# Expert weights in 4 MB transfers over a ring of four 32 KB places, in place of 2 MB transfers over nine 16 KB places

## The reference

```python
def expert(args):
    xb, e = args
    gu = (xb @ w_gu[e] + b_gu[e]).astype(f32)
    gate, up = jnp.split(gu, 2, axis=-1)
    gate = jnp.minimum(gate, SWIGLU_LIMIT)
    up = jnp.clip(up, -SWIGLU_LIMIT, SWIGLU_LIMIT)
    act = (up + 1.0) * gate * jax.nn.sigmoid(SWIGLU_ALPHA * gate)
    return act.astype(x.dtype) @ w_down[e] + b_down[e]
```

## Time and profile before

| | |
|---|---|
| median of 3 runs | 1506.49 us (1506.26 to 1506.98) |
| the profiled execution, time | 1506.73 us |
| its span, first to last instruction | 1505.0 us |
| PE busy / weight loads | 1466.1 us (97%) / 733.1 us (49%) |
| VectorE, ScalarE, GpSimd busy | 446.8, 344.2, 107.2 us |
| gate and up pieces | 128 transfers of 2048 KB, median 34.7 us from issue to landing |
| down pieces | 64 transfers of 2048 KB, median 35.9 us |
| bytes read from HBM | 491.19 MB (10^6 bytes) |
| granted TensorE clock, mean | 0.998 |

### The profile page before, as it was taken

One profiled execution on the slowest core, in us unless ns is written; L12 is line 12 of the kernel. 1 busy time (PEld: TensorE's weight loads), 2 busy tenths in 40 slices (PEclk: granted clock), 3 DMA queues, 4 the chain that ended last, 5 costly groups with the idle time before them and its releaser, 6 DMA issues.

```text
span 1505.0 us, 21866 instructions
## 1 busy us (share of the span) xinstructions
PE 1466.1 (97%) x8602; PEld 733.1 (49%) x8602; DVE 446.8 (30%) x918; ACT 344.2 (23%) x863; POOL 107.2 (7%) x95
## 2 busy tenths in 40 slices
PE   9999999999999999999999999999999999999997
PEld 7777776556777764333333333333333333333332
DVE  3653778776410137201101111111111101101113
ACT  1224215631210023212212112122112111211213
POOL 1003231010503301000000000000000000000000
PEclk9999999999999999999999999999999999999999
DMA  6346697546369767999999999999999999999996
GB/s 214 112 165 181 218 291 247 180 135 197 100 213 297 287 275 286 422 418 430 427 428 427 429 429 427 430 427 430 427 430 427 430 426 431 426 430 427 430 427 263
DMA packets 110574, 507.75 MB, mean 337 GB/s; under 512 B 12548, under 2 KB 49012, under 8 KB 85844
## 3 DMA queue, kind: packets, MB, share of 16 engines
q1 hardware_dynamic: 103840, 499.64, 82.9%
q10 hardware_dynamic: 6676, 7.29, 1.6%
HBM read 491.19 MB, written 15.72 MB: 337 GB/s over the span
## 4 chain that ended last, share of the span: by engine, by line
PE 67%; DMA 21%; DVE 3%; ACT 1%; issue 1%; DVEq 0%; SPq 0%; ACTq 0%
DMA wGU<-in_w_gu 21%; PE ps L2491 16%; PE ps L1950 12%; PE ps L2496 8%; PE ps L2259 4%; PE ps L2432 4%; PE ps L1966 3%; PE ps L2479 3%; PE ps L2483 3%; PE ps L2276 2%; PE ps L2289 2%; PE ps L2397 2%; PE ps L2413 1%; DVE up L1843 1%; DVE up L1842 1%; PE ps L2034 1%
## 5 line engine op out<-in xcount | busy, mean ns | idle before, releaser
L2491 PE MATMUL ps<-wGU,xe 128*64 128x512 f32 x1536 | 343.7, 595 | 15.7 <-DMA wGU<-in_w_gu 15.7
L2496 PE MATMUL ps<-wD,aT 128*64 128x512 f32 x1024 | 226.8, 595 | 0.0
L2491 PEld LDWEIGHTS ps<-wGU,xe 128*64 128x64 f32 x1536 | 108.4, 137 | 237.9 <-issue 211.3
L1950 PE MATMUL ps<-xT,ring 128*128 128x288 f32 (+1 forms) x848 | 179.6, 409 | 0.7 <-PEq L200 0.7
L1839 DVE TENSOR_SCALAR sg<-sg 128x512 f32<-128x512 f32 x32 | 13.7, 427 | 558.2 <-ACT sg L1280 558.2
L1950 PEld LDWEIGHTS ps<-xT,ring 128*128 128x128 f32 (+1 forms) x848 | 126.0, 172 | 44.6 <-issue 3.6
L2496 PEld LDWEIGHTS ps<-wD,aT 128*64 128x64 f32 x1024 | 71.4, 137 | 133.0 <-issue 126.2
L1280 ACT ACTIVATE sg<-ps 128x512 f32<-128x512 f32 x32 | 19.1, 597 | 487.2 <-PE ps L2479 487.2
L1229 ACT ACTIVATE xe<-ps,lnT 128x64 f32<-128x64 f32 x262 | 81.1, 420 | 1.2 <-PE ps L2406 1.2
L402 PE MATMUL ps<-xT,ring 128*128 128x288 f32 x320 | 78.1, 407 | 0.0
L1296 ACT COPY ysb<-ps 64x512 f32<-64x512 f32 x64 | 37.1, 579 | 155.5 <-PE ps L2496 154.8
(11 more groups left out here) (487 smaller groups left out, 1419.4 us busy)
## 6 DMA issues: line engine op xcount, KB each, us to landing
wGU<-in_w_gu SPq DMA_DIRECT2D x128, 2048.0 KB, 34.7
wD<-in_w_down SPq DMA_DIRECT2D x64, 2048.0 KB, 35.9
ring<-in_w_in SPq DMA_DIRECT2D x21, 2048.0 KB, 9.1
out<-hst SPq DMA_DIRECT2D x8, 1024.0 KB, 5.7
ringS<-in_ssd_proj SPq DMA_DIRECT2D x4, 2048.0 KB, 8.4
wbuf<-prompt_A_rows ACTq DMA_DIRECT2D x16, 384.0 KB, 3.8
out<-Sb SPq DMA_DIRECT2D x2, 2048.0 KB
ring<-in_hg_proj SPq DMA_DIRECT2D x2, 2048.0 KB, 8.6
```

What stands on the lines that cost most here:

```text
L1950: last = m.matmul(ps[h, b, 0:T], ring[c % 2][:, k, n * P + h.start:n * P + h.stop], xT[:, k, :], start=(k == 0), stop=(k == KD - 1))
L2491: last = m.matmul(ps[half[h], bank, :], xe[:, f, hx, :], wgu[n][:, k, col + CW * h:col + CW * h + CW], start=(i == 0 and k == 0), stop=False)
L2496: last = m.matmul(ps[half[h], B_Y, :], aT[:, k, i - 4, :], wdn[n][:, k, CW * h:CW * h + CW], start=False, stop=(i == 5 and k == 3))
```

## The change

Gate and up weights of a block are loaded as two transfers of 4 MB (512 rows each, four rows and 32 KB for each partition: `rows_4mb`); the two down pieces stay 2 MB. The ring has four places of 32 KB (`PAIRS = 4`), each of which takes one 4 MB transfer or two down pieces, in turn over the three places that a block needs (`pairs_of`). A fifth place (at 166 KB) is used once, for block 1. Four transfers of block 1's and two of block 2's gate and up weights keep 2 MB (`rows_2mb`, runs of 16 KB). A 4 MB transfer waits until both halves of its place are used. PE waits once for both halves (`LANDED` holds None for the second). Still, `m_f` counts every half as one piece. The loop body holds four blocks in place of six.

With the piece numbers of above, the refills wait for: pieces 10 to 13 for `m_f` = 1 to 4 (2 MB each, as before); 14+15 for 6; 16 for 7; 17 for 8; then, for every block b from 3 on, pieces 0+1 for 6(b - 1), pieces 2+3 for 6(b - 1) + 2, piece 4 for 6(b - 1) + 3, piece 5 for 6(b - 1) + 4.

Feature order follows: with four rows in each partition, `turn_x` takes every fourth value of `xs`; for block 0, `first_rows` writes its gather in the other order, and `lng4` is loaded in four transfers whose runs are 8 bytes.

```diff
-RING = 9
+PAIRS = 4
...
-        buf_kb = (64, 80, 116, 132, 32, 48, 0, 16, 166, 182)
-        wgu = [at(f"wGU{i}", kb, [P, 2, 2 * D]) for i, kb in enumerate(buf_kb)]
-        wdn = [at(f"wD{i}", kb, [P, 4, D]) for i, kb in enumerate(buf_kb)]
+        pair_kb = (64, 116, 32, 0, 166)
+        wgu = [at(f"wGU{i}", kb, [P, 4, 2 * D]) for i, kb in enumerate(pair_kb)]
+        wdn = [at(f"wD{i}", pair_kb[i // 2] + 16 * (i % 2), [P, 4, D]) for i in range(2 * PAIRS)]
...
+        def pairs_of(b):
+
+            if b < 2:
+                return ((0, 1, 2), (3, 4, 0))[b]
+            return tuple((3 * (b - 2) + 1 + j) % PAIRS for j in range(3))
...
+                def rows_4mb(e, g, p, sem):
+
+                    sp.dma_start(wgu[p][:], w_gu[0, bass.ds(e, 1), CW * g:CW * g + CW, :].rearrange("a (p k) n -> p (a k) n", p=P)).then_inc(sem, 16)
...
-                sp.dma_start(lng4[0:4, :], ln1_g[0].rearrange("(r n) -> r n", n=256)).then_inc(t_wr, 16)
-                sp.dma_start(lng4[4:8, :], ln1_b[0].rearrange("(r n) -> r n", n=256)).then_inc(t_wr, 16)
+                for h in range(2):
+                    sp.dma_start(lng4[0 + 2 * h:2 + 2 * h, :].rearrange("i (p k) -> i p k", k=2),
+                                 ln1_g[0, CW * h:CW * h + CW].rearrange("(p i k) -> i p k", i=2, k=2)).then_inc(t_wr, 16)
+                for h in range(2):
+                    sp.dma_start(lng4[4 + 2 * h:6 + 2 * h, :].rearrange("i (p k) -> i p k", k=2),
+                                 ln1_b[0, CW * h:CW * h + CW].rearrange("(p i k) -> i p k", i=2, k=2)).then_inc(t_wr, 16)
...
-                e = expert(sp, 1)
-                for g in range(RING + 1, 24):
-                    if g in (12, 18):
-                        e = expert(sp, g // 6)
-                    sp.wait_ge(m_f, g - RING if g < 2 * RING + 1 else g - RING + 1)
-                    piece(e, g % 6, (g - 1) % RING, m_w[(g - 1) % RING])
+                e = expert(sp, 1)
+                for j in range(2):
+                    sp.wait_ge(m_f, 1 + j)
+                    down(e, j, j, m_w[j])
+                e = expert(sp, 2)
+                for j in range(2):
+                    sp.wait_ge(m_f, 3 + j)
+                    rows_2mb(e, j, 1, m_h if j else m_w[2])
+                sp.wait_ge(m_f, 6)
+                rows_4mb(e, 1, 2, m_w[4])
+                for j in range(2):
+                    sp.wait_ge(m_f, 7 + j)
+                    down(e, j, 6 + j, m_w[6 + j])
+
+                def load(e, b, used):
+
+                    p, q, d = pairs_of(b)
+                    sp.wait_ge(m_f, used)
+                    rows_4mb(e, 0, p, m_w[2 * p])
+                    sp.wait_ge(m_f, used + 2)
+                    rows_4mb(e, 1, q, m_w[2 * q])
+                    for j in range(2):
+                        sp.wait_ge(m_f, used + (3 + j))
+                        down(e, j, 2 * d + j, m_w[2 * d + j])
...
-                        pe.wait_ge(m_w[n], loaded)
+                        if LANDED[base][i] is not None:
+                            n, loaded = LANDED[base][i]
+                            pe.wait_ge(m_w[n], turn0 * (16 if n % 2 else 48) + loaded)
```

More of the change, by code:

```diff
@@ L595, in build @@
         g_ln = S("ln_parameters_loaded")
-        m_w = [S(f"expert_piece_loaded{i}") for i in range(RING + 1)]
+        m_w = [S(f"expert_piece_loaded{i}") for i in range(2 * PAIRS + 2)]
+        m_h = S("second_half_of_first_refilled_gate_rows_loaded")
         m_re, m_ok = S("first_experts_reloaded"), S("first_experts_right")
@@ L722, in expert, with four, landings @@
             return eng.value_load(tab[0:1, bass.ds(b, 1)], min_val=0, max_val=E_ - 1)
-        def six(eng, it, left, body, r=0):
-            with eng.If(it * 6 + r < left):
+        def four(eng, it, left, body, r=0):
+            with eng.If(it * 4 + r < left):
                 body(it, r)
-                if r < 5:
-                    six(eng, it, left, body, r + 1)
+                if r < 3:
+                    four(eng, it, left, body, r + 1)
+        def pairs_of(b):
+            if b < 2:
+                return ((0, 1, 2), (3, 4, 0))[b]
+            return tuple((3 * (b - 2) + 1 + j) % PAIRS for j in range(3))
+        def landings():
+            count, table = [0] * (2 * PAIRS + 2), []
+            for b in range(6):
+                p, q, d = pairs_of(b)
+                sems = (2 * p, 2 * p + 1, 2 * q, 2 * q + 1, 2 * d, 2 * d + 1) if b == 1 else (2 * p, None, 2 * q, None, 2 * d, 2 * d + 1)
+                row = []
+                for n in sems:
+                    if n is not None:
+                        count[n] = count[n] + 1
+                    row.append(None if n is None else (n, 16 * count[n]))
+                table.append(row)
+            return table
+        LANDED = landings()
         def gathered(k):
@@ L852, in _ @@
                     sp.dma_start(ring[n][:], hg_proj[0].rearrange("(k p) n -> p k n", p=P)[:, :, CW * n:CW * n + CW]).then_inc(s_w[n], 16)
-                for i in range(2, 4):
-                    piece(0, i, i, m_w[i])
+                rows_4mb(0, 1, 1, m_w[2])
                 for n in range(2):
@@ L880, in _ @@
                     e = expert(sp, 1)
-                    for i in range(6, RING + 1):
-                        sp.wait_ge(m_w[i], 16)
-                        piece(e, i - 6, i, m_re)
+                    for i in range(4):
+                        sp.wait_ge(m_w[6 + i], 16)
+                        rows_2mb(e, i, 3 + i // 2, m_re)
                     sp.wait_ge(m_re, 16 * 4)
@@ L1300, in _ @@
                 with act.Fori(0, TURNS) as it:
-                    six(act, it, end - 1, lambda it, r: run(it * 6 + (r + 2), r % 2 == 1))
+                    four(act, it, end - 1, lambda it, r: run(it * 4 + (r + 2), r % 2 == 1))
                 a.activation(fvar[:, 7:8], ident[:, 0:1], ACT.Sqrt)
@@ L1860, in _ @@
                 run(1, True, 1)
-                with turns(dve, 0, TURNS, (dstep, 33)) as it:
-                    six(dve, it, end - 1, lambda it, r: run(it * 6 + (r + 2), r % 2 == 1))
+                with turns(dve, 0, TURNS, (dstep, 22)) as it:
+                    four(dve, it, end - 1, lambda it, r: run(it * 4 + (r + 2), r % 2 == 1))
                 lstep.on(dve)
@@ L2261, in _ @@
                     last.then_inc(g_s, 1)
-                pe.wait_ge(t_wr, 96)
+                pe.wait_ge(t_wr, 128)
                 m.transpose(ps[:, 0, 0:16], lngr[:], ident[0:16, 0:16])
@@ L2354, in first_rows @@
                         for h in range(2):
-                            c = CW * h + 256 * i
-                            sel, rows = (pselb[:], hp2[:, c:c + 256]) if t == 2 else (psel[:, t, :], xres[:, t, c:c + 256])
-                            last = m.matmul(ps[half[h], bank, 0:256], sel, rows, start=(t == 2), stop=(t == 1))
+                            c = slice(CW * h, CW * h + CW)
+                            sel, rows = (pselb[:], hp2[:, c]) if t == 2 else (psel[:, t, :], xres[:, t, c])
+                            last = m.matmul(ps[half[h], bank, 0:256].rearrange("q (p k) -> q p k", k=2), sel,
+                                            rows.rearrange("r (p i k) -> r i p k", i=2, k=2)[:, i], start=(t == 2), stop=(t == 1))
                         if t == 1:
@@ L2432, in prompt, with run @@
                     return m.matmul(ps[:, ACC[j], :], gT[:, t * P:(t + 1) * P], ysb[j % 2][:], start=False, stop=stop)
-                def run(b, turn0, first, odd, places=None, head=False):
+                def run(b, turn0, base, odd, head=False):
+                    pairs = pairs_of(base)
                     if not head:
@@ L2440, in run @@
                             pe.wait_ge(*((t_x0, 2), (t_xa, 1), (t_xa, 2), (m_xc, 1))[i])
-                        n, loaded = (first + i) % RING, turn0 * 64 + 16 * ((first + i) // RING + 1)
-                        if places is not None:
-                            n, loaded = places[i], 16 if i < 4 else 32
+                        w = wgu[pairs[i // 2]]
                         if i == 1 and not odd and not head:
@@ L2478, in run @@
                                 for h in range(2):
-                                    last = m.matmul(ps[half[h], B_G, :], xe[:, 2 + k, 1, :], wgu[n][:, k, CW * h:CW * h + CW], start=False, stop=(k == 1))
+                                    last = m.matmul(ps[half[h], B_G, :], xe[:, 2 + k, 1, :], w[:, 2 + k, CW * h:CW * h + CW], start=False, stop=(k == 1))
                             last.then_inc(m_u, 1)
@@ L2482, in run @@
                                 for h in range(2):
-                                    last = m.matmul(ps[half[h], B_U, :], xe[:, 2 + k, 1, :], wgu[n][:, k, D + CW * h:D + CW * h + CW], start=False, stop=(k == 1))
+                                    last = m.matmul(ps[half[h], B_U, :], xe[:, 2 + k, 1, :], w[:, 2 + k, D + CW * h:D + CW * h + CW], start=False, stop=(k == 1))
                             last.then_inc(m_f, 1)
@@ L2495, in run @@
```

(7 more changed lines are left out.)

46 lines of the change are left out of this document (23 added, 23 removed).

## The result

The changed kernel took **1515.49 us** (median of six runs, 1514.78 to 1517.11) beside 1506.39 us for the kernel before (six runs, 1506.10 to 1507.45): ratio 1.0059, 95% interval 1.0049 to 1.0069, so 9.1 us slower. Its profiled execution took 1515.06 us with a span of 1513.3 us; the span before was 1505.0 us. The two spans are 8.3 us apart.

The account below looks back on a forecast made before the run. The continuous DMA weight stream plus a tail was taken to bound the kernel. A 4.8 us later last landing (3.5 gained included) and 3.9 us longer tail made 8.7 us: 1515 us, own range 1511 to 1519.

Parts of the forecast that it names:

- Step 1: Loop transfers: 4 MB takes 9.73 us in place of 9.79 (bounds 9.68 to 9.79); 59 transfers, 3.5 us gained.
- Step 2: Early load stream: queue dry for 2.1, 5.7 and 1.5 us; last landing 4.8 us later, at 1491.8.
- Step 3: Kernel's end: PE ends its down pieces 7.9 us after the last landing, before 4.0; tail 3.9 us longer.
- Step 4: Loop's ring, PE waits of some 2 us and four-block body: nothing; `turn_x` at most some tenths of a us.
- Step 5: Layer norm loads before the mixer: four transfers with 8-byte runs take 8.5 us on two engines, hidden; nothing lost.
- The fixed cost of each transfer: Rival at 59 vanished seams between transfer halves: 0.29 us each gives 17 us back, 1498, not slower; chance 0.08.
- The change doesn't do what it says: Rival in the 4 MB transfers: runs go out as 16 KB, 1519; or 32 KB runs 1% slower, 1524; chance 0.08.
- The bare slope: Rival in the loop transfers: 32 KB runs stream at the pure slope or better, 1510 to 1512 us; chance 0.10.
- the late mixer: Rival before the mixer: `lng4` delays it by up to 7 us, total up to 1522; chance 0.07.
- The clock: Rival on PE: waits of some 2 us lower its clock, costing 20 to 34 us, 1535 to 1550; chance 0.05.
- The sum: Whole kernel: 4.8 us later last landing plus 3.9 us longer tail, 8.7 us, giving 1515 us, 0.6% slower.
- The rival: The clock rival on PE: waits of some 2 us lower its clock, costing 20 to 34 us; chance 0.05.

Follow-up runs that it names:

- two kernels with one median: Changed kernel with each 4 MB transfer as two of 2 MB waited for together, and with 4 MB transfers in runs of 16 KB: 1519.39 us each.
- fifth place: Changed kernel with its fifth 32 KB place kept in the ring until block 6, so refills of blocks 3 to 7 are released earlier: 1509.66 us.
- two waits: Changed kernel with each 4 MB transfer as two of 2 MB, PE waiting for each half before its piece, joint releases kept: 1515.46 us.
- each half released by itself: Changed kernel with gate and up weights in 2 MB transfers, each half released and waited for separately: 1512.45 us.

## Why the prediction was right

I predicted 1515 us and slower; it is 1515.5. Step by step:

- **Step 1, the transfer.** 9.73 us predicted, 9.71 measured, out of a range of 9.68 to 9.79. The cause is the length of the runs: the kernel with 4 MB in runs of 16 KB gave 9.79, the figure named for no gain. The fixed part of 7 ns a run is a line through two lengths that met a third within 0.02 us; what makes it, no run shows.
- **Step 2, the stream runs dry.** Predicted gaps 2.1, 5.7 and 1.5 us; measured about 1.5, 5.6 and 2.1 (a landing less 9.71 less the landing before it). Piece 23 was 9.7 us late, where 8.9 was predicted; the first two transfers of 4 MB on an empty queue took 12.3 and 12.2 us where I had 12.6, but the third took 12.8, and pieces 22 and 23 took 10.3 us between them where I had 9.8. I had one queue and one rule (landing before, or issue + 2.9), and it placed three gaps within 0.6 us. The last landing came 3.5 us late and not 4.8: 0.8 more at piece 23, but the 28 blocks after it took 818.2 us and not 819.0 and 1.3 of strays, which I had carried over from before.
- **Step 3, the tail.** 7.9 us after the last landing predicted, 7.8 measured, and 7.9 against 4.0 in the pair of kernels that differ in the wait alone.
- **Step 4, the ring and PE's waits.** PE's waits from 1000 us on are what was said, longer and fewer, and none at pieces 1 and 3:

```profile
PE ps L2543 <- DMA wGU<-in_w_gu: 22.6, 15, 2.0
```

  They are 22.6 us in 15 waits, against 15.7 in 23, and the stream's pace did not change with it. What I had not priced is the end: 1.0 us between the last down matmuls and the end of the span. The chain of the kernel before has this as its last item:

```profile
1501.75 0.66 DVEq L755
```

  The same item is nearly as far from the last down matmuls in both (1509.81 - 1498.25 = 11.6 us, 1502.41 - 1490.97 = 11.4 before), so 0.9 of it lies in the last store: 1513.3 - 1509.81 = 3.5 us against 1505.0 - 1502.41 = 2.6. Among the DMA queues from 1495 us to the end is one that fetches instructions (packets, MB, share of 16 engines):

```profile
q14 instruction: 2, 0.02, 0.3%
```

  and of the kernel before from 1490 us to its end, which has no other queue in it:

```profile
q1 hardware_dynamic: 719, 1.19, 20.3%
```

  Two fetches of instructions fall into the tail, the later one at 1510.2, beside the last store. All kernels made from the changed one have 15.0 to 15.4 us here and two fetches, or three (the one with 15.4); the kernel before and the one made from it have 14.0 and none. "Neither its branches nor its fetches lie on the stream; nothing" was thus true of the stream and 1 us off at the end. That the fetch delays the store is read from the times; no run takes it away, and it stays open.
- **Step 5, `lng4`.** The four transfers on SP (ns, min/median/max, and starts of the first and the last), then SP's timeline:

```profile
L874 SPq DMA_DIRECT2D lng<-in_ln_g x2: 288/2875/5462, 469.9 to 470.2; - x2
L877 SPq DMA_DIRECT2D lng<-in_ln_b x2: 880/955/1030, 475.7 to 476.6; - x2
...
477.77 0.77 SPq L836 DMA_DIRECT2D ringS<-in_ssd_proj  x1
DMA to landing us min/median/max: 8.2/8.2/8.2
492.99 15.89 SPq L886 DMA_DIRECT2D ring<-in_hg_proj  x2
```

  The four transfers held SP itself for 7.8 us, where I had looked at the engines only. That was 0.3 us too long: `ringS` went out at 477.77, right behind them and 0.3 us later than before. It landed at 486.0, 0.6 us later, and `hg_proj` went out within 0.05 us of its old time, so it cost nothing. The size was off: the 1024 packets of 8 bytes ran from 475.3 to 479.3 us, 3.9 us where I had 8.5. And "enough even if all 8.5 fell behind 477" does not follow from my own rows, since 8.5 is 1.0 more than the 7.5 of cover; the smaller size hid this.
- **The rivals.** The fixed cost of each transfer is refuted by two kernels with one median. "The change doesn't do what it says" is out, as runs of 32 KB and of 16 KB differ by 3.9 us. The bare slope and the late mixer are out by the rows above. The clock did fall, and "2 us is still short" was wrong for two waits; its price was far too high (last section).
- **The sum** was luckier than its parts: 1.3 us too much at the last landing and 1.0 missing at the end nearly cancel.

## What to carry to other kernels

The stream of queued loads that bounds this kernel gained nothing from fewer transfers and little from longer runs. So, for such a stream, price first what the larger unit takes: a place fewer in the ring, a release and a wait that come together, each read from the issue times and the chain before. Such a loss can be set far from where PE waits, in a stretch where PE is busy all the time, so look at GB/s in windows and not only at waits. If larger transfers are wanted, keep the release and the last block's waits fine, and keep every place in the ring while the lead lasts.

## What the runs showed of the hardware

In the changed kernel the granted clock fell twice after 1000 us (at 1150.8 and 1266.8), each time for a part of one piece and behind a wait of PE of about 2 us. A window of it, and PE's timeline at the first fall:

```profile
1150.80:1154.10 3.30, 3.30 (x10) 1.20 (x8) 0.00 (x0) 0.00 (x0) 0.00 (x0) 0.50 1.06 457
```

```profile
1149.69 5.35 PE L2543 MATMUL ps<-wGU,xe 128*64 128x512 f32 x16 [2.05 <-DMA wGU<-in_w_gu]
```

0.50 is the 1.2 GHz level. PE made 15 waits after 1000 us; six of them took 1.87 to 2.05 us, and four of these six were not followed by a fall. A piece took 5.35 us in place of 3.65, and then PE, which has some 5% to spare in this stretch, caught up: nothing of it reached the end. That depends on where the fall comes. In two of the other kernels one came in the last block but one, at 1445.20 (4 MB in runs of 16 KB) and 1436.15 (fifth place), and PE took up piece 2 of the last block 0.4 and 0.8 us after its landing, where it does so within 0.05 us in the changed kernel. The rival had the mechanism right and its price far too high. The three kernels whose longest wait for a landing was 1.1 us (before, two waits, each half released by itself) showed no fall between 585 us and the last down matmuls.

A DMA issue can hold the issuing engine for long, and not by its form alone: four transfers of 256 runs of 8 bytes each took 0.29, 5.46, 0.88 and 1.03 us on SP, where most transfers of 2 MB take 0.33. The 5.46 ended at 475.7, and the first of their packets ran at 475.3, so it may have been a wait for the transfers ahead in the queue; no run shows which. The prediction had counted them on the DMA engines only.
